# Where the tensors of a matmul-bound transformer kernel begin in on-chip memory: weight tiles at 0, moving data at 192 modulo 256 bytes of a partition

## The chip, the cores and the metric

The kernel runs on one core of one Trainium2 chip. The metric is the time on the device in microseconds (us) of one execution. Lower is better. The kernel before was executed three times for the comparison, and once more under the profiler, from which all durations below come.

## The reference

Two stacks of layers are computed one after the other on a sequence of 256 tokens of width 1024, in float32, with batch 1. The first stack has two layers, each of a SwiGLU feed-forward part, a mixer (dilated window attention beside a linear recurrent unit in the first layer, a gated delta rule in the second), cross attention to 256 memory tokens, and a second feed-forward part. The second stack has four layers: retention, a convolution block, gated linear attention and retention again, each followed by an MLP of width 4096 with a squared ReLU. Cut to what costs time:

```python
x = x + 0.5 * swiglu(rmsnorm(x), w_in, w_out)        # 1024 -> 2 x 2816 -> 1024, four times
x = x + mixer(rmsnorm(x), ...)                       # projections 1024 -> 1024 and wider
x = x + cross_attention(rmsnorm(x), rmsnorm(mem), wq, wkv, wo)
...
h = h + rmsnorm(mixer_2(rmsnorm(h)))                 # retention, convolution, gla, retention
h = h + rmsnorm(square(relu(u @ w_up)) @ w_down)     # 1024 -> 4096 -> 1024, four times
```

Nearly all of the work is the product of 256 tokens with weight matrices that are each used once. All weights together are 835 tiles and more of 512 KB, some 440 MB.

## The kernel before, in words

**Weights.** A host function lays the weights out as tiles of 128 partitions by 1024 float32 columns, each tile of four blocks of 128 x 256. `sync_program` moves them in order into a ring of seven buffers `SL0` to `SL6` (line 2912). ScalarE rounds a tile to the reduced format fp32r into a ring of five buffers `WH0` to `WH4` (`hi`, line 2087), and VectorE writes the remainder, tile minus rounded tile, to `WL0` to `WL6` (`lo`, line 1007). `WLi` is another name for the bytes of `SLi`: the remainder overwrites the tile it came from.

**Moving data.** The activations are kept transposed (features on partitions, 256 tokens in a row for each 128 features) and are split in the same way into a rounded and a remaining part. These parts lie in `RB`, `R03`, `R45` and `R67`, which are other names for the bytes of `BIG` and of the pages `PG0` to `PG7`.

**TensorE.** Every matrix product goes through `mm` (line 270), `mm(out, left, right)`: `left`, 128 columns, is loaded into the array first (LDWEIGHTS), and `right` is streamed past it (MATMUL). In `multiply`, for each block of 128 x 256 weights and each of its two halves of 128 columns, three matmuls accumulate in PSUM: rounded weights with rounded data, rounded weights with remaining data, remaining weights with rounded data. So in nearly all matmuls the weight tile is loaded (128 columns, 512 bytes of a partition) and the data is streamed (256 columns, 1024 bytes). Every matmul has its own load, two in a row from `WH` and one from `WL`. In `multiply_tok`, which serves the few products whose result has tokens on the partitions, it is the other way round: the data is loaded and 512 columns of a weight tile are streamed. The remaining matmuls (attention, norms, convolution, the delta rule) are in plain float32, each issued to the array as two instructions.

**What sets the order.** The order is written out by hand. Each engine walks through the same table of stages. TensorE waits for a tile's remainder (`s_lo`), ScalarE rounds tile t when TensorE is through with tile t - 5, and the transfer of tile t starts when TensorE is through with tile t - 7. Everything is released by counts of finished blocks (`s_block`), not by time.

**Where the tensors begin.** The tensors are allocated one behind the other in the order of the lines in `build_program`. Each start is rounded up to 32 bytes, and the first of them, `XG`, begins at byte 16512 of each partition. All sizes but those of `XG` (8256 bytes), `RST` (1032 bytes) and `PK` (4756 bytes) are multiples of 256 bytes. The names that share bytes (`WL`, `RB`, `R03`, `R45`, `R67`) are allocated in a scope of their own, which is left before `SL`, `BIG` and `PG` are allocated over the same place. That gives these starts modulo 256 bytes:

| tensor | before | after the change |
|---|---|---|
| XG | 128 | 128 |
| H | 192 | 192 |
| SL, WL (tiles from DMA, remaining part of the weights) | 192 | 0 |
| BIG, PG, RB, R03, R45, R67 (moving data), CP, RST | 192 | 192 |
| RT2, ONES, POS, PK | 224 | 224 |
| WH (rounded part of the weights) | 128 | 0 |

Inside a tile, the 128 columns of one load begin at a multiple of 512 bytes from the tile's start, and the 256 columns of one stream at a multiple of 1024 bytes from the start of the data. So the table holds for each single load and stream.

Of the kernel before, what the change touches and what calls it, by code (L numbers as in the profile page):

```python
# [112 lines left out]
def build_program(nc, w, pk, cp, xT_in, mem_in, pos_in, out):  # L113
    F32 = mybir.dt.float32
# [12 lines left out]
    with ctx:  # L127
        def sb(name, n, dt=F32):
            return ctx.enter_context(nc.sbuf_tensor(name, [128, n], dt))
# [4 lines left out]
        XG = sb("XG", 2064)  # L134
        X = XG[:, 16:2064]
        H = sb("H", 2048)
        with ExitStack() as names:
            WL = [names.enter_context(nc.sbuf_tensor(f"WL{i}", [128, 1024], F32R)) for i in range(NRAW)]
            RB, R03, R45, R67 = (names.enter_context(nc.sbuf_tensor(n, [128, c], F32R))
                                 for n, c in (("RB", 8192), ("R03", 8192), ("R45", 4096), ("R67", 4096)))  # L140
        SL = [sb(f"SL{i}", 1024) for i in range(NRAW)]
        BIG = sb("BIG", 8192)
        PG = [sb(f"PG{i}", 2048) for i in range(12)]
        CP = sb("CP", 1536)
# [4 lines left out]
        ONES = sb("ONES", 128)  # L149
        POS = sb("POS", 256, I32)  # L150
        PK = sb("PK", NPK)
        WH = [sb(f"WH{i}", 1024, F32R) for i in range(NSPL)]
        BK = [ctx.enter_context(nc.psum_tensor(f"B{i}", [128, 512], F32)) for i in range(8)]

        def pc(name, a=0, n=1):
            o = COLS[name][0] + a
            return PK[:, o:o + n]

# [12 lines left out]
        def cc(c):  # L171
            return slice(c * 256, (c + 1) * 256)

        IDN = PK[:, COLS["ident"][0]:COLS["ident"][0] + 128]
        RB2 = RST[:, 0:256].unsqueeze(1).broadcast_to([128, 2, 256])
# [87 lines left out]
        def diag_room(x):  # L263
            tile_ = (H, PG[11], PG[4], PG[5], PG[2], PG[3])[x // 16] if x < 96 else BIG
            at = x % 16 * 128 if x < 96 else 2304 + (x - 96) * 128
            return tile_[:, at:at + 128]

        def tensor_program(p):
            def mm(o, left, right, first=True, final=True):
                return p.matmul(o, left, right, start=first, stop=final, skip_group_check=True)  # L270
# [9 lines left out]
            def keep(n):  # L280
# [4 lines left out]
                for _ in range(n):  # L285
                    mm(BK[b][:, 0:256], IDN, PK[:, 0:256])

# [7 lines left out]
            def tile(st, j, k):  # L295
# [3 lines left out]
                elif b == 1 or b % 4 == 0:  # L299
                    p.wait_ge(s_lo, b // 4 + 1)  # L300
                return WH[b // 4 % NSPL], WL[b // 4 % NRAW], b % 4 * 256

# [96 lines left out]
            def normed(name, n=None):  # L399

                st = ST[name]

                def lower(j, k):
                    if j == 0:
                        p.wait_ge(h_lo.sem, h_lo[n, k])
                for j, k in gemm(name, R67, R67, 0, 2048, None if n is None else lower):
                    if n is not None and (j, k) == ((3, 0) if st.outer else (1, 0)):
                        total(n)
                    if n is not None and j == 0:
                        p.wait_ge(h_hi.sem, h_hi[n, k])  # L410
                    yield j, k

            def through(blocks):
                for jk in blocks:
                    pass
# [32 lines left out]
            def attn_lru():  # L448
                Q, K = PG[2][:, 0:1024], PG[2][:, 1024:2048]
                VV = PG[3][:, 0:1024]  # L450
                XC = H[:, 0:1024]
                S0, S1 = BIG[:, 0:1024], BIG[:, 1024:3072]
                PT0, PT1 = PG[8], BIG[:, 3072:4096]
                through(normed("ab.q", 1))
# [108 lines left out]
            def deltanet():  # L563
                U = CP[:, 0:128]
                WIDE, QT, VB, KB = PG[1], PG[2], PG[9], PG[8]
                L, LT, Y, YT, M1 = H, PG[1], PG[5], PG[4], H
                UU, WT, KN, ZT = PG[5], BIG[:, 2048:4096], PG[0], H[:, 0:1024]

# [3 lines left out]
                def part(base, x):  # L572
                    at = base + x % 8 * 256 + x // 8 * 128
                    return BIG[:, at:at + 128]

# [12 lines left out]
                def gates():  # L588
                    bk = small("dab")
                    p.wait_ge(full.sem, full[5, 7])  # L590
                    for tb in range(2):
                        for k in range(8):
                            t = mm(bk[:, tb * 16:(tb + 1) * 16], H[:, k * 256 + tb * 128:k * 256 + (tb + 1) * 128],
                                   pc("wab", k * 16, 16), k == 0, k == 7)
# [204 lines left out]
            def conformer():  # L799
                HP = BIG[:, 0:8 * 286].rearrange("p (c t) -> p c t", t=286)  # L800
                Cv, csq = PG[1], PG[10]
# [51 lines left out]
            def gla():  # L853
# [68 lines left out]
                for j, k in normed("g.qk", 17):  # L922
                    if (j, k) == (3, 4):
                        bk = small("gt1")
                        p.wait_ge(full.sem, full[17, 7])
                        for c in range(8):
                            t = mm(bk[0:32, 0:256], pc("gw1", c * 32, 32), H[:, cc(c)], c == 0, c == 7)
                        t.then_inc(s_small, 1)
# [74 lines left out]
        def vector_program(v):  # L1003
            def lo(t):
                if t < NTILES:
                    v.wait_ge(s_hi, t + 1)
                    v.tensor_tensor(WL[t % NRAW][:, :], SL[t % NRAW][:, :], WH[t % NSPL][:, :].bitcast(F32),  # L1007
                                    ALU.subtract).then_inc(s_lo, 1)

            def lo_part(part, needs, gives):  # L1010
                v.wait_ge(needs, 1)
                v.tensor_tensor(WL[0][:, part], SL[0][:, part], WH[0][:, part].bitcast(F32), ALU.subtract).then_inc(gives, 1)

# [1067 lines left out]
        def scalar_program(a):  # L2081
            def hi(t):
                if t < NTILES:
                    a.wait_ge(s_w[t % NRAW], 16 * (t // NRAW + 1))
                    if t >= NSPL:
                        a.wait_ge(s_block, 4 * (t - NSPL + 1))
                    a.activation(WH[t % NSPL][:, :], SL[t % NRAW][:, :], ACT.Copy).then_inc(s_hi, 1)  # L2087

            def hi_part(part, needs, gives):
                a.wait_ge(needs, 16)  # L2090
                a.activation(WH[0][:, part], SL[0][:, part], ACT.Copy).then_inc(gives, 1)

# [772 lines left out]
        def sync_program(s):  # L2865
# [28 lines left out]
            def piece(x):  # L2894
                at = slice(16 + XCUT[x] * 256, 16 + XCUT[x + 1] * 256)
                s.dma_start(XG[:, at], xT_in[:, at]).then_inc(s_x[x], 16)

            s.dma_start(SL[0][:, 0:256], w[0][:, 0:256]).then_inc(s_w_first, 16)
            s.dma_start(SL[0][:, 256:1024], w[0][:, 256:1024]).then_inc(s_w[0], 16)
            piece(1)  # L2900
            again = {ST["f2.0.in"].block // 4 + 8: (1, "xo0"), ST["f2.1.in"].block // 4 + 8: (2, "xo1"),
                     ST["m1.up"].block // 4 + 8: (3, "r0.o"), ST["m2.up"].block // 4 + 8: (2, "g.o")}
            for t in range(NTILES):
# [11 lines left out]
                if t == 3:  # L2915
                    s.dma_start(PK[:, :], pk).then_inc(s_pk, 16)
                if t == 6:
# [181 lines left out]
```

## Time and profile before

| | us |
|---|---|
| median of 3 runs | 2770.7 (2767.42 to 2773.44) |
| the profiled execution, whole | 2767.97 |
| its span | 2766.2 |
| TensorE, matmuls (PE) | 2689.7 busy, 97% of the span |
| TensorE, loads (PEld) | 2601.1 busy, 94% |
| VectorE (DVE) | 1819.0 busy, 66% |
| ScalarE (ACT) | 1409.9 busy, 51% |
| mean granted TensorE clock | 0.996 of full |

The busy time of a matmul is from its start to its modelled end, and neighbouring matmuls overlap in the array. So the mean duration of a matmul is much longer than the distance from one start to the next. What a matmul costs in a dense stretch is that distance, called the pace below.

### The profile page before, as it was taken

The numbers are of one execution on the slowest core, as the hardware profiler recorded it, in microseconds if no ns is written. First come the engines' busy times: TensorE is split into PE (matmuls) and PEld (weight loads), VectorE is DVE, ScalarE is ACT, GpSimd is POOL, SyncE is SP. The second block draws the span as 40 slices with busy tenths as digits, with TensorE's granted clock in tenths as the row PEclk, the third lists the DMA queues.
The fourth block names the chain that finished last, engine by engine and source line by source line (L and its number), as shares of the span: only waits on it lengthen the run. The fifth ranks groups of instructions, "written<-read, shape, count | busy, mean of one in ns | idle before, by whom it ended". The sixth has DMA issues, their size and how long they took to land. (4 is left out here: it accounts for less than half of the span.)

```text
span 2766.2 us, 49224 instructions
## 1 busy us (share of the span) xinstructions
PE 2689.7 (97%) x21088; PEld 2601.1 (94%) x21088; DVE 1819.0 (66%) x2374; ACT 1409.9 (51%) x1935; POOL 0.2 (0%) x4
## 2 busy tenths in 40 slices
PE   8999999999998899999999999989999999999998
PEld 8999999999987889999999999979988999989998
DVE  6658766656667656666756856878554785756764
ACT  5445654454466355544446565454454544446543
POOL 0000000000000000000000000000000000000000
PEclk9999999999999999999999999999999999999999
DMA  6554545555543234555544555235543555544553
GB/s 243 176 189 158 171 149 187 187 184 188 185 142 114 70 130 142 196 185 175 183 145 153 181 185 172 73 115 180 189 148 107 170 187 186 170 159 150 171 185 128
DMA packets 129865, 450.12 MB, mean 163 GB/s; under 512 B 20208, under 2 KB 21104, under 8 KB 129520
## 3 DMA queue, kind: packets, MB, share of 16 engines
q1 hardware_dynamic: 129504, 446.83, 48.3%
q8 instruction: 167, 2.74, 0.4%
q14 instruction: 50, 0.41, 0.1%
q10 hardware_dynamic: 144, 0.14, 0.0%
HBM read 445.48 MB, written 1.44 MB: 162 GB/s over the span
## 5 line engine op out<-in xcount | busy, mean ns | idle before, releaser
L270 PE MATMUL B<-R,WH 128*128 128x256 f32 x10432 | 2083.5, 283 | 17.2 <-DVE R L1222 8.5
L270 PEld LDWEIGHTS B<-R,WH 128*128 128x128 f32 x10432 | 1676.8, 188 | 30.4 <-issue 10.9
L1007 DVE TENSOR_TENSOR WL<-SL,WH 128x1024 fp32r<-128x1024 f32 x835 | 1007.9, 1223 | 721.9 <-ACT WH L2087 721.0
L270 PE MATMUL B<-R,WL 128*128 128x256 f32 x4480 | 1262.5, 282 | 0.0
L2087 ACT ACTIVATE WH<-SL 128x1024 fp32r<-128x1024 f32 x835 | 863.2, 1052 | 522.8 <-PE B L270 512.3
L270 PEld LDWEIGHTS B<-R,WL 128*128 128x128 f32 x4480 | 845.5, 189 | 0.0
L270 PE MATMUL B<-RB,WH 128*128 128x256 f32 x1984 | 553.8, 279 | 0.0
L270 PE MATMUL B<-RB,WL 128*128 128x256 f32 x1728 | 487.2, 282 | 0.0
L270 PEld LDWEIGHTS B<-RB,WH 128*128 128x128 f32 x1984 | 373.3, 188 | 0.1
L270 PEld LDWEIGHTS B<-RB,WL 128*128 128x128 f32 x1728 | 325.2, 188 | 0.0
L270 PE MATMUL B<-WH,R 128*128 128x512 f32 x480 | 158.1, 401 | 0.0
L270 PE MATMUL B<-PG 128*128 128x256 f32 (+6 forms) x672 | 129.1, 336 | 7.0 <-DVE PG L1532 3.8
L270 PEld LDWEIGHTS B<-PG 128*128 128x128 f32 (+2 forms) x672 | 105.6, 186 | 20.9 <-DVE PG L1521 3.5
L2622 ACT ACTIVATE RB<-PG 128x512 fp32r<-128x512 f32 x64 | 40.5, 633 | 165.0 <-DVE PG L1678 165.0
L270 PEld LDWEIGHTS B<-WH,R 128*128 128x128 f32 x480 | 90.2, 188 | 25.3 <-issue 3.5
L2167 ACT ACTIVATE R<-XG,PK 128x256 fp32r<-128x256 f32 x120 | 57.8, 505 | 92.0 <-DVE XG L1153 50.3
L270 PE MATMUL B<-WL,R 128*128 128x512 f32 x240 | 95.4, 398 | 0.0
L2274 ACT ACTIVATE RB<-PG 128x512 fp32r<-128x512 f32 x44 | 27.8, 632 | 131.5 <-DVE PG L1199 131.5
L270 PE MATMUL B<-PG,ONES 128*128 128x256 f32 (+1 forms) x188 | 58.5, 426 | 27.2 <-DVE PG L1058 9.0
L1126 DVE TENSOR_TENSOR R<-PG,RB 128x512 fp32r<-128x512 f32 x108 | 73.9, 684 | 3.3 <-ACT RB L2274 2.8
L2271 ACT ACTIVATE PG<-PG 128x512 f32<-128x512 f32 x44 | 27.8, 633 | 88.7 <-DVE PG L1192 88.7
L1092 DVE SCALAR_TENSOR_TENSOR R<-XG,PK,R 128x256 fp32r<-128x256 f32 x120 | 55.4, 482 | 21.0 <-ACT R L2167 21.0
(293 smaller groups left out, 1566.6 us busy)
## 6 DMA issues: line engine op xcount, KB each, us to landing
SL<-in_w SPq DMA_DIRECT2D x835, 512.0 KB, 3.3
CP<-in_cp SPq DMA_DIRECT2D x5, 768.0 KB, 4.9
PG<-in_mem SPq DMA_DIRECT2D x1, 1024.0 KB, 12.9
PK<-in_pk SPq DMA_DIRECT2D x1, 594.5 KB, 9.4
XG<-in_xT SPq DMA_DIRECT2D x1, 512.0 KB, 7.9
out<-XG SPq DMA_DIRECT2D x1, 512.0 KB, 2.6
SL<-in_w SPq DMA_DIRECT2D x1, 384.0 KB, 3.5
XG<-in_xT SPq DMA_DIRECT2D x1, 256.0 KB, 6.3
```

The costliest lines, as they stand in the source:

```text
L270: return p.matmul(o, left, right, start=first, stop=final, skip_group_check=True)
L1007: v.tensor_tensor(WL[t % NRAW][:, :], SL[t % NRAW][:, :], WH[t % NSPL][:, :].bitcast(F32), ALU.subtract).then_inc(s_lo, 1)
L1092: v.scalar_tensor_tensor(R67[:, 2048 + c * 256:2304 + c * 256], X[:, cc(c)], gain(c), R67[:, cc(c)].bitcast(F32), ALU.mult, ALU.subtract). ...
L1126: v.tensor_tensor(R03[:, hc(u)], d, RB[:, hc(u)].bitcast(F32), ALU.subtract).then_inc(hid_lo.sem, hid_lo.give((f, u)))
L2087: a.activation(WH[t % NSPL][:, :], SL[t % NRAW][:, :], ACT.Copy).then_inc(s_hi, 1)
L2167: a.activation(R67[:, cc(c)], X[:, cc(c)], ACT.Copy, scale=gain(c)).then_inc(h_hi.sem, h_hi.give((n, c)))
L2271: a.activation(s, s, ACT.Silu).then_inc(silu.sem, silu.give((f, u)))
L2274: a.activation(RB[:, hc(u)], PG[10][:, u % 4 * 512:u % 4 * 512 + 512], ACT.Copy).then_inc(hid_hi.sem, hid_hi.give((f, u)))
L2622: a.activation(RB[:, hc(x)], PG[10][:, x % 4 * 512:x % 4 * 512 + 512], ACT.Copy).then_inc(hid_hi.sem, hid_hi.give((f, x)))
```

## The change

Four tensors that nothing reads or writes are added. `ROOM0` (16 columns, 64 bytes) moves everything behind `H`. `ROOM` and `ROOM1` (48 columns, 192 bytes each, at the same place in the two scopes) lie between the tiles and the moving data. `ROOM2` (32 columns, 128 bytes) lies ahead of `WH`. No instruction is added, removed or reordered, and no operand has another shape; only start addresses differ. The starts that result modulo 256 bytes are in the table above.

```diff
         H = sb("H", 2048)
+        sb("ROOM0", 16)
         with ExitStack() as names:
             WL = [names.enter_context(nc.sbuf_tensor(f"WL{i}", [128, 1024], F32R)) for i in range(NRAW)]
+            names.enter_context(nc.sbuf_tensor("ROOM", [128, 48], F32))
             RB, R03, R45, R67 = (names.enter_context(nc.sbuf_tensor(n, [128, c], F32R))
                                  for n, c in (("RB", 8192), ("R03", 8192), ("R45", 4096), ("R67", 4096)))
         SL = [sb(f"SL{i}", 1024) for i in range(NRAW)]
+        sb("ROOM1", 48)
         BIG = sb("BIG", 8192)
...
         PK = sb("PK", NPK)
+        sb("ROOM2", 32)
         WH = [sb(f"WH{i}", 1024, F32R) for i in range(NSPL)]
```

## Rows read from the trace of the kernel before

**Rows 1.** The page's busy times: engine, us, share of the span, instructions.
```profile
PE 2689.7 (97%) x21088; PEld 2601.1 (94%) x21088; DVE 1819.0 (66%) x2374; ACT 1409.9 (51%) x1935; POOL 0.2 (0%) x4
```

**Rows 2.** The page's costliest groups: out<-in xcount, busy us, mean ns, idle before.
```profile
L270 PE MATMUL B<-R,WH 128*128 128x256 f32 x10432 | 2083.5, 283 | 17.2 <-DVE R L1222 8.5
...
L270 PE MATMUL B<-R,WL 128*128 128x256 f32 x4480 | 1262.5, 282 | 0.0
...
L270 PE MATMUL B<-RB,WH 128*128 128x256 f32 x1984 | 553.8, 279 | 0.0
L270 PE MATMUL B<-RB,WL 128*128 128x256 f32 x1728 | 487.2, 282 | 0.0
...
L270 PE MATMUL B<-WH,R 128*128 128x512 f32 x480 | 158.1, 401 | 0.0
...
L270 PE MATMUL B<-WL,R 128*128 128x512 f32 x240 | 95.4, 398 | 0.0
```

**Rows 3.** Windows, dense 256-column stretches: us, PE, PEld, DVE, ACT, POOL, PEclk, DMA.
```profile
415.00:585.00 170.00, 170.00 (x1446) 170.00 (x1445) 106.96 (x115) 80.32 (x94) 0.00 (x0) 1.00 0.55 186
600.00:780.00 180.00, 180.00 (x1527) 179.82 (x1526) 116.02 (x123) 86.16 (x105) 0.00 (x0) 1.00 0.56 186
1130.00:1290.00 160.00, 160.00 (x1361) 160.00 (x1360) 108.14 (x128) 75.94 (x92) 0.00 (x0) 1.00 0.56 187
```

**Rows 4.** Timeline of PE from 1200 us: start us, us, instruction, merged count.
```profile
1199.89 0.28 PE L270 MATMUL B<-R,WL 128*128 128x256 f32 x1
1200.00 0.40 PE L270 MATMUL B<-R,WH 128*128 128x256 f32 x2
1200.24 0.28 PE L270 MATMUL B<-R,WL 128*128 128x256 f32 x1
1200.36 0.40 PE L270 MATMUL B<-R,WH 128*128 128x256 f32 x2
```

**Rows 5.** Timeline of PE from 650 us.
```profile
649.79 0.40 PE L270 MATMUL B<-R,WH 128*128 128x256 f32 x2
650.02 0.28 PE L270 MATMUL B<-R,WL 128*128 128x256 f32 x1
...
651.20 0.40 PE L270 MATMUL B<-R,WH 128*128 128x256 f32 x2
```

**Rows 6.** Timeline of PEld, the loads, from 1200 us.
```profile
1199.89 0.30 PEld L270 LDWEIGHTS B<-R,WH 128*128 128x128 f32 x2
...
1200.24 0.30 PEld L270 LDWEIGHTS B<-R,WH 128*128 128x128 f32 x2
```

**Rows 7.** Windows: 512 columns; float32 with 256; float32 with 16.
```profile
1360.00:1395.00 35.00, 35.00 (x151) 28.03 (x150) 25.47 (x22) 17.26 (x19) 0.00 (x0) 1.00 0.53 182
1756.00:1796.00 40.00, 40.00 (x187) 35.01 (x186) 39.83 (x98) 7.27 (x18) 0.00 (x0) 1.00 0.00 1
793.00:796.00 3.00, 3.00 (x29) 3.00 (x28) 2.65 (x6) 1.76 (x3) 0.00 (x0) 1.00 0.60 180
```

**Rows 8.** Timeline of PE in the 512-column stretch, from 1360 us.
```profile
1359.68 0.62 PE L270 MATMUL B<-WH,R 128*128 128x512 f32 x2
1360.14 0.40 PE L270 MATMUL B<-WL,R 128*128 128x512 f32 x1
1360.38 0.63 PE L270 MATMUL B<-WH,R 128*128 128x512 f32 x2
...
1362.96 0.40 PE L270 MATMUL B<-WL,R 128*128 128x512 f32 x1
```

**Rows 9.** Groups by form: the float32 matmuls with 16 columns.
```profile
L270 PE MATMUL B<-PK,H 128*128 128x16 f32 x32 | 3.6, 260 | 0.0
```

**Rows 10.** Waits: engine, line, waited for, us in total, times, longest.
```profile
DVE WL L1007 <- ACT WH L2087: 721.0, 546, 7.1
ACT WH L2087 <- PE B L270: 512.3, 333, 8.3
```

**Rows 11.** DMA issues: KB each, median us to landing.
```profile
SL<-in_w SPq DMA_DIRECT2D x835, 512.0 KB, 3.3
```

## The prediction

> **What bounds the kernel now.** I read the page's busy times first. TensorE is busy for 97% of the span with matmuls and 94% with loads, VectorE for 66% and ScalarE for 51% [rows 1]. The waits say the same: VectorE's longest wait is for ScalarE, 721 us, and ScalarE's longest is for TensorE, 512 us [rows 10]. Both have slack, so a faster TensorE finds its tiles ready. The next question is which matmuls fill TensorE. Four groups with a weight tile loaded and 256 columns streamed hold 10432 + 4480 + 1984 + 1728 = 18624 matmuls, and 480 + 240 = 720 matmuls stream 512 columns of a weight tile [rows 2].
>
> Their mean duration of 0.28 us is no price, since they overlap. The price is the pace, start to start. A window counts every matmul that overlaps it, so I take off the duration over the pace, 0.28 / 0.118 = 2.4: 170 / 1443.6 = 117.8 ns from 415 to 585 us, 160 / 1358.6 = 117.8 ns from 1130 to 1290 us, and 180 / 1524.6 = 118.1 ns from 600 to 780 us, where one short pause falls in [rows 3]. [...] 18624 x 0.1178 = 2194 us, 79% of the span. The 720 take 35 / (151 - 1.7) = 0.2344 us each [rows 7], 169 us. The rest, about 400 us, is float32 matmuls and pauses between stages, which the change does not address.
>
> **What a pace of 117.8 ns is made of.** A load of the next weights starts together with each matmul: the pair of `WH` loads at 1199.89 us starts with the `WL` matmul, and the one at 1200.24 us again [rows 4, 6]. [...] Float32 matmuls with 16 columns have next to nothing to stream, and with a duration of 260 ns [rows 9] go at 3.00 / (29 - 2.3) = 0.112 us [rows 7]: the pace of loads alone. Float32 matmuls with 256 columns go at 40 / (187 - 1.75) = 0.216 us [rows 7]. [...]
>
> **The change part by part.** *ROOM0, ROOM and ROOM1, ROOM2 issue nothing.* No instruction, wait or transfer is added, and all counts stay. Their whole effect is on start addresses. *Moving data* (192) stays where it was modulo 256 bytes, and so do the float32 operands, so their price of 0 rests on an unchanged relation between them. *The weight tiles* go from 128 (`WH`) and 192 (`WL`) to 0. For the load beside a stream, the distance from data to weights goes from -64 and 0 to +64 bytes for all.
>
> Does the distance matter? In the 256-column stretches, the order of paces differs. Around 1200 us the step from a `WL` matmul to the next `WH` is 0.11 and 0.12 us, mean 115 ns, and a `WH` pair takes 0.24 us, 120 ns each [rows 4]. Around 650 us the rhythm is another, with 0.23 us for the first pair, but four triples take 651.20 - 649.79 = 1.41 us, 117.5 ns for each of the twelve [rows 5]. The mean is the same. [...]
>
> The 512-column matmuls are the only rows with the new distance. There the data is loaded (192) and the tile streamed, so weights from `WH` (128) are at +64 and from `WL` (192) at 0. A `WL` matmul takes 1360.38 - 1360.14 = 0.24 us. A `WH` pair takes 0.46 us, 0.23 each; over the stretch, five pairs and four singles take 3.28 us, which fits 0.232 and 0.24 [rows 8]. So the distance of +64 is 8 ns cheaper over 512 columns, or up to 4 over 256. The bounds for the new pace are 112 (loads alone) below and 120 (the slow step of rows 4) above. I take 115.0 ns, the quick step of rows 4, half way between now and the floor and within the 4 ns that rows 8 allow: 117.8 - 115.0 = 2.8 ns, x 18624 = 52.1 us less. The 512-column matmuls get the distance -64, for which they have no row: 0, with bounds of 5 ns either way, 720 x 5 = 3.6 us.
>
> *DMA, ScalarE and VectorE* read and write `SL`, `WL` and `WH` at the new starts. A tile lands in 3.3 us [rows 11] and seven are under way; a tile lasts TensorE 24 x 0.1178 = 2.8 us. I cost these at 0, covered by the waits of 721 and 512 us [rows 10]. Were the cover gone, 1% on the tile work of these engines would still be under 10 us.
>
> The sum: 2767.97 - 52.1 = 2715.9 us for the profiled execution. The median of the runs stands 2.7 us above it, so 2719 us. What is late next is still TensorE: with 2.76 us per tile, the other engines have over 1 us to spare.
>
> [...]
>
> **The rivals.** [...]
>
> *Slower.* Now the loads alternate between starts of 128 and 192, and the quick step follows the switch from `WL` to `WH` [rows 4]. With all tiles at 0 no switch is left, and every step may fall into the slow one of 120 ns. [...] Price: 2.2 x 18624 = 41.0 us, and 5.6 x 720 = 4.0 us if the 512-column ones all take the 240 ns of `WL`: 2771 + 45 = 2816 us. Against it: rows 8, where the new distance is the cheap one.
>
> [...]
>
> **How the numbers follow.** The forecast has a chance of 0.40, all of it 0.13, no change 0.29, slower 0.18. A measurement of this kernel can tell about 0.2%, 5.5 us, from no change. Faster is 0.53, same 0.29, slower 0.18. The forecast's own range is 2690 to 2745 us (paces of 113.4 to 116.4 ns). The range for 8 in 10 takes in no change and most of the way to the two outer cases: 2668 to 2788 us, with about 0.05 left out below and 0.15 above.
>
> **What would show it.** In the windows of rows 3, the count at 115.0 ns would be 1394 in 160 us of a dense stretch; unchanged is 1361, the slow case 1336, all of it 1431. The rhythm of rows 4 would lose the difference between `WL` and `WH` steps, since both tiles now start alike. The float32 pace of 0.216 and the 16-column pace of 0.112 must stay; if they move, something else than the distance acts. The 512-column pace tells whether -64 is dear. The forecast is wrong if the dense count is within 3 of the old one, or below it.

## The result, and the profile after

The changed kernel takes 2727.4 us (median of 4 runs, 2720.4 to 2736.2) where the kernel before takes 2771.9 us: ratio 0.984, interval 0.981 to 0.988. The profiled execution is 2720.4 us with a span of 2718.6 us, 47.6 us less than before. The single runs now lie 16 us apart; those of before lay 6 us apart. Four more runs of the same program, below, have a median of 2737.2 us, and all eight one of 2732.5, so the gain is nearer 38 us (1.4%) than 44.

The page's busy times and two of its groups (line numbers are 4 higher than before) answer to [rows 1, 2]:

```profile
PE 2637.8 (97%) x21088; PEld 2551.8 (94%) x21088; DVE 1817.6 (67%) x2374; ACT 1409.6 (52%) x1935; POOL 0.2 (0%) x4
...
L274 PE MATMUL B<-R,WH 128*128 128x256 f32 x10432 | 2043.8, 281 | 17.4 <-DVE R L1226 8.4
...
L274 PE MATMUL B<-R,WL 128*128 128x256 f32 x4480 | 1247.1, 279 | 0.0
```

TensorE is still busy for 97%, with the same counts, and the durations in these two groups are 2 and 3 ns shorter. VectorE's and ScalarE's busy times are unchanged, and their waits are shorter than those of [rows 10]. Waits of the changed kernel:

```profile
DVE WL L1011 <- ACT WH L2091: 684.4, 531, 8.6
ACT WH L2091 <- PE B L274: 473.1, 320, 8.3
```

So they lost slack and nothing else. The pace shows where the time came from. Windows of the changed kernel, columns as in [rows 3]; the last three answer to [rows 7] (512 columns, float32 with 256, float32 with 16):

```profile
80.00:200.00 120.00, 120.00 (x1021) 120.00 (x1020) 77.57 (x82) 55.26 (x65) 0.00 (x0) 1.00 0.57 187
420.00:580.00 160.00, 160.00 (x1414) 160.00 (x1413) 104.39 (x112) 75.86 (x88) 0.00 (x0) 1.00 0.58 194
1120.00:1270.00 150.00, 150.00 (x1326) 150.00 (x1325) 105.32 (x126) 73.36 (x88) 0.00 (x0) 1.00 0.59 193
2170.00:2310.00 140.00, 140.00 (x1237) 140.00 (x1237) 97.97 (x119) 69.36 (x83) 0.00 (x0) 1.00 0.58 194
2560.00:2700.00 140.00, 140.00 (x1191) 140.00 (x1190) 83.83 (x88) 60.85 (x68) 0.00 (x0) 1.00 0.53 174
1330.00:1365.00 35.00, 35.00 (x155) 28.71 (x154) 27.84 (x25) 17.26 (x19) 0.00 (x0) 1.00 0.58 188
1720.00:1760.00 40.00, 40.00 (x187) 35.00 (x187) 39.83 (x98) 7.73 (x18) 0.00 (x0) 1.00 0.00 1
775.00:777.00 2.00, 2.00 (x20) 2.00 (x20) 1.74 (x3) 1.54 (x3) 0.00 (x0) 1.00 0.59 201
```

With 2.4 taken off each count, the dense windows do not show one new pace. They show two: 160 / 1411.6 = 113.3 ns, likewise 113.3 from 1120 and from 2170 us, but 120 / 1018.6 = 117.8 ns from 80 us and 140 / 1188.6 = 117.8 ns from 2560 us. The slow pace is exactly the old one. The clock is 1.00 in all of them, and the float32 windows have their old paces (187 in 40 us again; 20 - 2.3 in 2 us, 0.113 each).

Single steps, timeline of PE in the changed kernel, first in a quick stretch, then in a slow one:

```profile
699.78 0.28 PE L274 MATMUL B<-R,WL 128*128 128x256 f32 x1
699.89 0.39 PE L274 MATMUL B<-R,WH 128*128 128x256 f32 x2
700.12 0.28 PE L274 MATMUL B<-R,WL 128*128 128x256 f32 x1
700.23 0.39 PE L274 MATMUL B<-R,WH 128*128 128x256 f32 x2
700.46 0.28 PE L274 MATMUL B<-R,WL 128*128 128x256 f32 x1
...
701.14 0.28 PE L274 MATMUL B<-R,WL 128*128 128x256 f32 x1
...
2599.89 0.28 PE L274 MATMUL B<-R,WL 128*128 128x256 f32 x1
2600.01 0.40 PE L274 MATMUL B<-R,WH 128*128 128x256 f32 x2
2600.24 0.28 PE L274 MATMUL B<-R,WL 128*128 128x256 f32 x1
```

In the quick stretch a triple takes 0.34 us (699.78 to 700.12, to 700.46; four in 1.36 us), in the slow one 0.35. There is no step of 0.12 us left in the quick one. The following comes from all start-to-start distances of the two traces, in stretches of at least 36 such matmuls without a step over 135 ns. In the changed kernel, 71% of these matmuls run in stretches at 113.3 ns and the others in stretches at 117.8 ns. From the twelfth step of a stretch on, each 24 matmuls of it have the same mean to 0.1 ns. In the trace of before, all stretches are at 117.8 ns, but there the single steps differ: around 1200 us they are 115 ns from `WL` to `WH`, 120 within the `WH` pair and 118 from `WH` to `WL`, and in most other stretches 121, 115 and 117. In the changed kernel the three are alike to about 1 ns at either pace.

Could VectorE or ScalarE, which read and write the same tiles, be what slows or quickens TensorE? In the long quick stretch from 410 us they come and go, and the pace does not follow. Two windows of it:

```profile
479.00:482.00 3.00, 3.00 (x29) 3.00 (x29) 2.58 (x3) 0.01 (x1) 0.00 (x0) 1.00 0.61 188
555.00:558.00 3.00, 3.00 (x29) 3.00 (x28) 1.69 (x3) 3.00 (x5) 0.00 (x0) 1.00 0.63 195
```

Cut into 130 pieces of 12 matmuls, this stretch has every piece at 113.2 to 113.4 ns each, while VectorE is busy for 9% to all of a piece and ScalarE for nothing to all of it. So what these two engines do is not what sets the pace within a stretch. The transfers were not separated in this way.

### The profile page after: what moved, and what is told of

The parts are those of the page before. It is cut to its first block and busy times, and to the rows that moved or that the text cites. A ratio compares the mean times of both kernels' runs of the same rounds, so it can differ in the third digit from the quotient of the medians.

```text
span 2718.6 us, 49224 instructions
## 1 busy us (share of the span) xinstructions
PE 2637.8 (97%) x21088; PEld 2551.8 (94%) x21088; DVE 1817.6 (67%) x2374; ACT 1409.6 (52%) x1935; POOL 0.2 (0%) x4
## 5 line engine op out<-in xcount | busy, mean ns | idle before, releaser
L274 PE MATMUL B<-R,WH 128*128 128x256 f32 x10432 | 2043.8, 281 | 17.4 <-DVE R L1226 8.4
L274 PE MATMUL B<-R,WL 128*128 128x256 f32 x4480 | 1247.1, 279 | 0.0
L274 PE MATMUL B<-RB,WL 128*128 128x256 f32 x1728 | 479.1, 277 | 0.0
L274 PEld LDWEIGHTS B<-PG,ONES 128*128 128x128 f32 x188 | 33.7, 201 | 39.5 <-issue 30.7
```

## The experiments

All kernels are the kernel before with other unused columns; the instructions are the same in all of them. "Distance" is the start of the weight tiles minus the start of the moving data, modulo 256 bytes; the starts follow from the sizes and the order of allocation, and no trace shows them. The edits are shown against the changed kernel. Paces are worked out from the windows as above.

**The same kernel again** (no edit).

> The changed kernel once more, unchanged. In its trace each unbroken stretch of 256-column matmuls keeps one of two paces, 113.3 or 117.8 ns, from its first steps on; 70% of these matmuls ran at the quick one. If the pace of a stretch follows from the program alone, the same stretches are quick here and the time is 2720 us again within 2 us. If it is settled by how the two reads happen to meet at the start of a stretch, other stretches are slow this time, the quick share lies between 50 and 90%, and the time between 2710 and 2740 us.

Four runs: 2737.2 us (2731.3 to 2751.3), against 13 runs of before at 2770.9 us, ratio 0.988 (0.985 to 0.991). Windows of the repeated run:

```profile
430.00:590.00 160.00, 160.00 (x1414) 160.00 (x1413) 103.08 (x111) 76.14 (x90) 0.00 (x0) 1.00 0.58 195
1130.00:1280.00 150.00, 150.00 (x1276) 150.00 (x1275) 102.07 (x122) 70.44 (x85) 0.00 (x0) 1.00 0.57 186
2180.00:2320.00 140.00, 140.00 (x1191) 140.00 (x1190) 97.15 (x118) 67.29 (x82) 0.00 (x0) 1.00 0.57 188
```

The MLP stretches around 1200 and 2250 us were quick in the first trace (1326 in 150 us, 1237 in 140 us) and are slow here (1276 and 1191), while the one at 430 us is quick again. Now 49% of the matmuls are quick (the expectation had at least 50), and the span is 2739.0 us, 20.4 us more. The change in share, 0.22 x 18340 x 4.5 ns = 18 us, explains most of it. So the pace of a stretch is not fixed by the program alone. In these two traces it is settled in the first steps of a stretch and then held. It does not look like pure chance either: of 52 stretches that can be paired by length, 39 took the same pace in both traces, among them the one around 100 us and the last long one, which were slow twice. The changing share goes with the spread of the times; only two executions of this program have a trace. The two reads of the expectation are the load of a weight tile and the stream of the data beside it; that they meet is my picture, and no run shows it.

**Three uniform starts: is it likeness, the absolute place, or the distance?**

```diff
# e2: weights 0, data 0
-            names.enter_context(nc.sbuf_tensor("ROOM", [128, 48], F32))
-        sb("ROOM1", 48)
-        sb("ROOM2", 32)
+        sb("ROOM2", 16)
# e3: weights 128, data 192
-        sb("ROOM0", 16)
+        sb("ROOM0", 48)
-            names.enter_context(nc.sbuf_tensor("ROOM", [128, 48], F32))
+            names.enter_context(nc.sbuf_tensor("ROOM", [128, 16], F32))
-        sb("ROOM1", 48)
+        sb("ROOM1", 16)
-        sb("ROOM2", 32)
# e4: weights 64, data 0
-        sb("ROOM0", 16)
+        sb("ROOM0", 32)
```

> Weight tiles and moving data all begin at 0 modulo 256 bytes (distance from data to weights 0, both tiles alike). Distance theory (+64 bytes is what lets the quick pace in): no stretch is quick, 117.8 ns everywhere, 2771 us. Likeness theory (what counts is that WH and WL begin alike, wherever): quick stretches as in the changed kernel, 2715 to 2740 us. Absolute theory (the tiles must begin at 0 modulo 256): also 2715 to 2740 us.

> Both weight tiles begin at 128, moving data stays at 192 (distance -64, both alike). Distance theory: slow everywhere, 2771 us. Likeness theory: quick stretches, 2715 to 2740 us. Absolute theory: slow, 2771 us.

> Both weight tiles begin at 64 and the moving data at 0 (distance +64 as in the changed kernel, other absolute starts). Distance theory: quick stretches, 2715 to 2740 us. Likeness theory: the same. Absolute theory: slow everywhere, 2771 us.

Against the same 13 runs of before: e2 2799.5 us (4 runs), ratio 1.010 (1.009 to 1.012); e3 2768.6 us (10 runs), 0.999 (0.998 to 1.000); e4 2739.7 us (4 runs), 0.989 (0.986 to 0.993). Windows of e2:

```profile
430.00:590.00 160.00, 160.00 (x1336) 160.00 (x1335) 98.16 (x105) 72.53 (x85) 0.00 (x0) 1.00 0.56 184
620.00:760.00 140.00, 140.00 (x1169) 140.00 (x1168) 90.62 (x95) 63.46 (x74) 0.00 (x0) 1.00 0.56 183
```

of e3:

```profile
430.00:590.00 160.00, 160.00 (x1361) 160.00 (x1360) 99.92 (x107) 72.78 (x85) 0.00 (x0) 1.00 0.56 187
1140.00:1280.00 140.00, 140.00 (x1238) 140.00 (x1237) 98.77 (x118) 69.30 (x84) 0.00 (x0) 1.00 0.58 195
```

of e4:

```profile
80.00:200.00 120.00, 120.00 (x1021) 120.00 (x1021) 77.61 (x82) 55.65 (x65) 0.00 (x0) 1.00 0.56 186
430.00:590.00 160.00, 160.00 (x1414) 160.00 (x1414) 102.56 (x110) 77.24 (x91) 0.00 (x0) 1.00 0.59 194
```

e2 goes at 120.0 ns in every stretch: the tiles are alike and begin at 0, and yet it is the slowest of the four. Both the likeness and the absolute theory fall. e4 shares only the distance of +64 with the changed kernel, and it has its two paces (52% quick) and its time. The distance theory is the one that is left, but two of its numbers failed. For e2 it wanted 117.8 ns and 2771 us, and distance 0 costs 120.0 ns and 2799.5 us. And e3 at -64 is not wholly slow: 11% of its matmuls are at 113.3 ns (x1238 in 140 us), where the theory wanted none.

**Each part alone.** e5 leaves out ROOM2 (WL 0, WH 128: distances +64 and -64). e6 keeps ROOM2 alone (WL 192, WH 0: distances 0 and +64).

```diff
# e5
-        sb("ROOM2", 32)
# e6
-        sb("ROOM0", 16)
-            names.enter_context(nc.sbuf_tensor("ROOM", [128, 48], F32))
-        sb("ROOM1", 48)
```

> One part alone: SL and WL begin at 0 as in the changed kernel, WH stays at 128 (ROOM0, ROOM and ROOM1 without ROOM2). Every third load is then at distance +64, the others at -64. If the quick pace needs one distance for all three matmuls of a triple, no stretch is quick: 117.8 ns, 2771 us. If each matmul profits by itself, dense stretches go at 117.8 - 4.4 / 3 = 116.3 ns, 2743 us.

> The other part alone: WH begins at 0, SL and WL stay at 192 (ROOM2 alone). Two of three loads are at distance +64, one at 0, which cost 120.0 ns where all had it. If the quick pace needs one distance for all, 117.8 ns or more and 2771 us or more. If each matmul counts by itself, (2 x 113.3 + 120.0) / 3 = 115.5 ns and 2728 us.

One run each, beside a run of before at 2773.9 us: e5 2755.4, e6 2772.8 us. Windows of e5:

```profile
80.00:200.00 120.00, 120.00 (x1062) 120.00 (x1061) 79.19 (x85) 56.74 (x68) 0.00 (x0) 1.00 0.57 194
430.00:590.00 160.00, 160.00 (x1349) 160.00 (x1347) 98.53 (x106) 71.60 (x83) 0.00 (x0) 1.00 0.54 186
```

of e6:

```profile
430.00:590.00 160.00, 160.00 (x1360) 160.00 (x1360) 99.96 (x107) 72.70 (x85) 0.00 (x0) 1.00 0.56 186
```

Neither expectation for e5 came out: 34% of its matmuls are at 113.3 ns and the others at 118.9, slower than before. Each matmul does not profit by itself, but one distance for all is not needed for the quick pace either. Nor is the pace always held to the end here: two stretches, from 317 and from 409 us, turn from 118.9 to 113.3 ns without a pause for their last 40 matmuls. e6 has no quick stretch, as its first expectation said, and two short ones at 122 ns. The two parts do not add up: -18 us and -1 us here, against -44 or -34 us together (the parts are single runs, but their paces say the same). Three kernels have WL at 192, on the start of the data (before, e2 and e6), and none of them has a quick stretch.

**The remaining distances, and the period.** Only the unused columns differ (uniform weights at 64, 32, 224, 160 and 96, data at 192). e11 has 64 more columns ahead of each part:

```diff
# e11 (e7 to e10 and e12 change the same four numbers)
-        sb("ROOM0", 16)
+        sb("ROOM0", 80)
-            names.enter_context(nc.sbuf_tensor("ROOM", [128, 48], F32))
+            names.enter_context(nc.sbuf_tensor("ROOM", [128, 112], F32))
-        sb("ROOM1", 48)
+        sb("ROOM1", 112)
-        sb("ROOM2", 32)
+        sb("ROOM2", 96)
```

> Both weight tiles at 64, moving data at 192: distance +128. If the placing repeats every 256 bytes and the far side of a row is best, all stretches are quick: 113.3 ns, 2690 us. If it repeats every 128 bytes, distance 128 is distance 0 again: 120.0 ns everywhere, 2799 us.

> Both weight tiles at 32, moving data at 192: distance +96. If the cost falls in steps of 64 bytes, +96 behaves as +64: stretches at 113.3 and 117.8 ns, 2710 to 2750 us. If it changes in finer steps, a pace that no run has shown yet, between 113.3 and 120.0 ns.

> Both weight tiles at 224, moving data at 192: distance +32, between 0 (120.0 ns in every stretch) and +64 (113.3 or 117.8 ns). If placing acts in steps of 64 bytes, one of its two neighbours' pictures. If it acts smoothly, stretches between 117 and 120 ns and about 2780 us, as at +96. If the best place lies between, more matmuls at 113.3 ns than the 50 to 70% of +64 and under 2720 us.

> Both weight tiles at 160, moving data at 192: distance -32, between -64 (117.8 ns, a tenth of the matmuls at 113.3) and 0 (120.0 ns). Smooth: 118 to 120 ns and about 2785 us. Steps of 64 bytes: as -64 or as 0.

> The same starts modulo 256 bytes as in the changed kernel, with 64 more columns ahead of the weight tiles, ahead of the moving data and ahead of WH, so that the weights move by 256 and 768 bytes and the data by 512. The loads' distance to the data is then the same modulo 256 and another by 256 bytes modulo 512. If 256 bytes is the period: stretches at 113.3 and 117.8 ns only, 2710 to 2750 us. If the period is longer: other paces.

> Both weight tiles at 96, moving data at 192: distance -96, the last of the eight places 32 bytes apart. If only +64 and -64 admit the quick pace of 113.3 ns, no stretch has it here, and the time is 2750 to 2800 us. If it admits the quick pace in more stretches than +64 does, or holds one pace under 115 ns in all stretches, it is under 2720 us and better than the changed kernel.

One run each, beside runs of before at 2773.9 (e7, e8), 2769.3 (e9 to e11) and 2767.1 us (e12). Windows of e7, distance +128:

```profile
80.00:200.00 120.00, 120.00 (x1014) 120.00 (x1013) 77.33 (x81) 55.23 (x65) 0.00 (x0) 1.00 0.53 185
430.00:590.00 160.00, 160.00 (x1335) 160.00 (x1335) 99.04 (x107) 72.24 (x84) 0.00 (x0) 1.00 0.54 182
```

Windows of e8, +96:

```profile
430.00:590.00 160.00, 160.00 (x1366) 160.00 (x1365) 100.94 (x108) 73.45 (x86) 0.00 (x0) 1.00 0.54 187
```

Windows of e9, +32:

```profile
430.00:590.00 160.00, 160.00 (x1354) 160.00 (x1354) 100.16 (x107) 72.26 (x85) 0.00 (x0) 1.00 0.54 186
```

Windows of e10, -32:

```profile
430.00:590.00 160.00, 160.00 (x1374) 160.00 (x1373) 100.19 (x106) 73.98 (x86) 0.00 (x0) 1.00 0.54 190
```

Windows of e11, +64 again:

```profile
80.00:200.00 120.00, 120.00 (x1061) 120.00 (x1060) 79.27 (x84) 56.70 (x68) 0.00 (x0) 1.00 0.57 194
1140.00:1280.00 140.00, 140.00 (x1191) 140.00 (x1191) 93.55 (x113) 65.16 (x78) 0.00 (x0) 1.00 0.55 187
```

Windows of e12, -96:

```profile
430.00:590.00 160.00, 160.00 (x1336) 160.00 (x1335) 98.93 (x106) 71.94 (x85) 0.00 (x0) 1.00 0.54 182
```

Put together, with the time of the median or the single run, and the paces of the stretches (shares of the matmuls in stretches of 36 or more). A single run can be off by the 7 us or so that runs of before lie apart, or by up to 30 us where the quick share varies:

| distance | kernel | us | paces, ns |
|---|---|---|---|
| -96 | e12 | 2802.6 | 120.0 |
| -64 | e3 | 2768.6 | 117.8; 113.3 (11%) |
| -32 | e10 | 2752.4 | 116.7 (96%); 117.8 |
| 0 | e2 | 2799.5 | 120.0 |
| +32 | e9 | 2776.5 | 118.3 |
| +64 | changed, e1, e4, e11 | 2727.4, 2737.2, 2739.7, 2726.7 | 113.3 (71, 49, 52, 63%); 117.8 |
| +96 | e8 | 2780.0 | 117.3; 118.7; 120.0 |
| +128 | e7 | 2791.9 | 118.7; 120.0 |
| WH -64, WL +64 | e5 | 2755.4 | 118.9; 113.3 (34%) |
| WH +64, WL 0 | e6 | 2772.8 | 117.8; 122 (1%) |
| WH -64, WL 0 | before | 2771.9 | 117.8 |

e7 refutes both of its theories: +128 is not the best place, and it is not quite distance 0. The steps of 64 bytes fail at e8, e9 and e10; e8 shows the paces between, 117.3 and 118.7 ns, that its second expectation asked for. The smooth picture fits e9 (118.3 ns, 2776.5 us) and fails at e10, where -32 has a better pace than 0 and, but for a tenth of the matmuls, than -64. e12 has no quick stretch, as its first expectation said, but at 2802.6 us lies just outside the 2750 to 2800 us. e11 has the paces and the time of the changed kernel, so moving all tensors by 256 bytes or multiples of it, in different numbers, changes nothing that can be seen. Of the eight places, +64 is the best on average. -32 is the one that is quicker than before in nearly all stretches (96% at 116.7 ns), but it gives less. No run beat the changed kernel beyond the spread of its own runs.

## Why the prediction was right, and where it was not

**The bound and the lever: right.** The rest of the kernel did not move, and the pace of the 256-column matmuls did. Their mean pace went from 117.8 to 114.7 ns; I had 115.0. Summed over the trace from start to next start, the groups of [rows 2] with 256 columns went from 2277.7 to 2229.0 us. The pace gave 3.04 ns x 18340 = 55.8 us (predicted 52.1). Steps over 135 ns took back 7.0 us: what they last beyond 117.8 ns went from 84.1 to 91.1 us, which I had cost at nothing. Half of that lies in time at a granted clock of 0.50, of which this trace has 42.6 us and that of before 24.3; how much of it the change brings about is not shown. The 512-column matmuls gave 2.5 us (predicted 0) and the remainder took 3.5. That makes 47.7 us against 52.1, and 2727 against 2719 us for the medians (2732.5 for all eight runs).

**One pace of 115 ns for all: wrong.** No stretch runs at 115.0. The value is a mean over two paces that each stretch keeps, and 113.3 is the floor that is reached. The mark I had set for the dense window, 1394 in 160 us, is met nowhere: it is 1414 in the quick stretches and 1361 in the slow ones. So the size came out by a mixture that I had not foreseen, and it differs from run to run. That it fell so near 115.0 ns is luck. The other mark was met: with all tiles at one start, the difference between `WL` and `WH` steps of [rows 4] is gone. The share of quick matmuls was 71, 49, 52 and 63% in four traces at +64.

**The floor: nearly right.** I took 112 ns, the pace of float32 loads with next to nothing streamed [rows 7]. The float32 matmuls of `mm` with 128 x 128 weights start 112 ns apart (median) with 128 columns as with 16, in the traces of both kernels, and 216 ns apart with 256. So up to 128 columns it is not the width of the stream that sets their step. That it is the load, and that an fp32r load costs the same, was my estimate: no run has loads alone. The quick pace is 113.3 ns. Timeline of PEld in the changed kernel, beside the matmul starts at 699.89 and 700.12 above:

```profile
700.12 0.30 PEld L274 LDWEIGHTS B<-R,WH 128*128 128x128 f32 x2
700.35 0.19 PEld L274 LDWEIGHTS B<-R,WL 128*128 128x128 f32 x1
700.46 0.30 PEld L274 LDWEIGHTS B<-R,WH 128*128 128x128 f32 x2
```

Each load again starts with a matmul (700.12, 700.46), and the next matmul starts 0.11 us later. That the load bounds the quick pace fits these numbers, but it is argued and not shown. The record of a load lasts 0.19 us here and in [rows 6], longer than a step, so the rows do not show what the next matmul waits for. What an fp32r stream of 256 columns costs without its load is not shown by any run either. So my limit on the gain, 112 ns and not less, is an estimate; the quickest that the runs showed for 256 columns is 113.3 ns.

**The argument from the 512-column rows: wrong, though its conclusion held.** I read from [rows 8] that a distance of +64 is 8 ns cheaper than 0. Here too, distance is loaded operand minus streamed one. Windows of e2 (distance 0), of e3 (+64, both tiles) and of the repeated run (-64):

```profile
1375.00:1410.00 35.00, 35.00 (x156) 29.00 (x155) 27.61 (x24) 16.90 (x20) 0.00 (x0) 1.00 0.58 195
1352.00:1387.00 35.00, 35.00 (x152) 28.05 (x151) 26.40 (x23) 16.45 (x19) 0.00 (x0) 1.00 0.56 189
2386.00:2421.00 35.00, 35.00 (x152) 28.35 (x151) 27.15 (x24) 16.75 (x19) 0.00 (x0) 1.00 0.57 189
```

By their starts, the dense stretches of 512 columns go at 226.8 ns in e2 and at 233.3 ns in e3. So for them +64 is the dearer one, by 6.5 ns. At -64 they go at 228.9 ns in every stretch of the first trace of the changed kernel, against 234.5 before, but in two of the five stretches of the repeated run at 233.3: they have two paces as well. The single steps of 0.24 and 0.232 us that I read in [rows 8] are no price of a distance, since all-0 gives 226.8. That +64 is good for 256 columns does not follow from rows 8. Of the other six uniform distances that were tried beside +64 and 0, only -32 is clearly quicker than before, so a part of the right direction is luck too. The other half of the argument, that paces of 115 and 120 ns exist with the same instructions [rows 4], pointed the right way. What picks between those two is not shown.

**The rivals.** "No change" (2771 us, a chance of 0.29) would have been right for a distance of -64 (e3) and for the WH part alone (e6). What refutes it for the fp32r matmuls is that with equal instructions and uniform starts their pace is 113.3 to 120.0 ns. For the float32 matmuls it holds: their 0.216 us stayed, also for the 32 of them between `H` and `BIG`, whose starts lie 64 bytes apart in e2 and e4 and are alike before. "Slower, everything at 120 ns" is the picture of e2 and e12, for another distance: I had priced it 45 us above before, and it measures 29 and 35. "All of it" (112 ns in every stretch, a chance of 0.13) is nearly reached in the quick stretches, at 113.3 ns, and in no kernel as a whole.

**What stays open.** Why a stretch takes one pace or the other is not shown. No run here controlled the moment at which a stretch starts. That the distance decides which paces occur is shown by the runs: 113.3 ns in four traces of four at +64, and 120.0 ns alone at 0 (e2) and at -96 (e12). That this is because the read of the load and the read of the stream meet in memory is my picture of it, with no experiment behind it. Why +64 is the best, and why -32 has a pace of its own, 116.7 ns, is open too. What the two rounded and remaining halves of the moving data would do at different starts was not tried.

## What to carry to other kernels

When matmuls of one shape, each with a load of its own, start at uneven distances in a dense stretch (115 and 120 ns here), or further apart than matmuls with next to nothing to stream (117.8 against 112 ns here), look at where the two operands begin modulo 256 bytes. The order of allocation sets this by accident, and here the best and the worst place are about 2.5% of the whole kernel apart. Before a change of layout is credited or blamed, profile it more than once: a mean pace can hide two steady ones, and one program's executions lay up to 31 us apart here. And take such a place from a measurement with the same shapes, since the 512-column matmuls were quickest at distance 0 (226.8 ns), where the 256-column ones are slowest (120.0 ns).

## What the runs showed of the hardware that was not expected

- In the changed kernel, unbroken stretches of the same instructions hold one of two paces, 113.3 or 117.8 ns, for up to 1583 matmuls, and the choice differs between executions of one program.
- The kernel before holds three different rhythms of single steps (two of them in [rows 4, 5]), all with a mean of 117.8 ns. With all weight tiles at one start the difference between steps is gone in the changed kernel (alike to about 1 ns) and in e2 (120.0 ns for every kind of step), but not in e12 (118 to 122 ns, mean 120.0).
- One fp32r matmul of 256 columns with its load costs 113.3, 116.7, 117.3, 117.8, 118.3, 118.7, 118.9 or 120.0 ns with the same instructions. Only the start addresses differ between the kernels: 113.3 ns occurs at +64, at -64 and in e5, and 120.0 ns at -96, 0, +96 and +128.
- The pace does not follow what VectorE and ScalarE do meanwhile: 113.2 to 113.4 ns in all 130 pieces of one stretch.
